# A hybrid delta-rule, attention and convolution trunk: value transposes one place later, and the weight splits of the first projection in mid-chunk

## What is computed

```
qkv_a, z_a, b_a, g_a, q_b, k_b, v_b, z_b = split_sizes(h @ w_in, AB_SIZES)
qkv_a = silu(causal_depthwise_conv(qkv_a, conv_w))
n_mat = where(strict, (k*beta) @ k.T * gamma, 0)          # 64 x 64 in each chunk of tokens
sol   = triangular_solve(eye + n_mat, [v*beta, k*beta*exp(decay)])
u, w  = sol[..., :dv], sol[..., dv:]
v_new = u - w @ state ;  o = q_dec @ state + qk @ v_new   # chunk after chunk
state = state * chunk_decay + k_dec.T @ v_new
```

## Time and profile before

| what | value |
|---|---|
| median of 3 runs | 2443.97 us (2443.47 to 2444.28) |
| span of the profiled execution | 2442.8 us; the launch's own time lies about 1.2 us above it (by the median) |
| TensorE busy | 2388.3 us, 98% of the span |
| DVE, ACT, GpSimd busy | 1294.1, 810.8, 229.8 us |
| longest chain | PE 83%, DVE 8%, issue 4%, ACT 2%, DMA 2% |
| DMA | 94 GB/s over the span |

### The profile page before, as it was taken

One profiled execution on the slowest core, in us unless ns is written; L12 is line 12 of the kernel. 1 busy time (PEld: TensorE's weight loads), 2 busy tenths in 40 slices (PEclk: granted clock), 3 DMA queues, 4 the chain that ended last, 5 costly groups with the idle time before them and its releaser, 6 DMA issues.

```text
span 2442.8 us, 29646 instructions
## 1 busy us (share of the span) xinstructions
PE 2388.3 (98%) x11652; PEld 1984.9 (81%) x11652; DVE 1294.1 (53%) x1725; ACT 810.8 (33%) x1377; POOL 229.8 (9%) x161
## 2 busy tenths in 40 slices
PE   7999999999999999999999999999999999999998
PEld 6788888888777878988777788888888888888776
DVE  5665656563555557643385783344333343433755
ACT  4233333332443436532244432212221222322434
POOL 3010101010010101001140420000000000001400
PEclk9999999999999999999999999999999999999999
DMA  6632333343433434452222233332323322333222
GB/s 174 109 70 67 76 68 75 66 77 70 123 91 73 83 73 131 149 180 96 93 70 69 78 97 94 103 103 81 108 86 103 103 95 86 95 104 121 69 69 86
DMA packets 237516, 229.80 MB, mean 94 GB/s; under 512 B 22384, under 2 KB 230768, under 8 KB 237424
## 3 DMA queue, kind: packets, MB, share of 16 engines
q1 hardware_dynamic: 236224, 226.96, 34.0%
q10 hardware_dynamic: 1200, 1.57, 0.2%
HBM read 223.52 MB, written 4.98 MB: 94 GB/s over the span
## 4 chain that ended last, share of the span: by engine, by line
PE 83%; DVE 8%; issue 4%; ACT 2%; DMA 2%; SPq 1%; POOL 0%; DVEq 0%; ACTq 0%; POOLq 0%
PE acc L887 22%; PE acc L889 21%; PE acc L888 21%; PE acc L1216 2%; PE acc L1217 2%; PE acc L1221 2%; DVE weights_lo L1353 2%; DMA weights_raw<-in_ab_w_in 1%; PE m L1036 1%; ACT weights_hi L460 1%; DVE work L1834 1%; PE acc L1089 1%; PE acc L1090 1%; PE acc L1091 1%; PE m L966 1%
## 5 line engine op out<-in xcount | busy, mean ns | idle before, releaser
L887 PE MATMUL acc<-input_hi,weights_hi 128*128 128x512 f32 (+1 forms) x2776 | 1092.1, 393 | 16.1 <-DVE weights_lo L1353 14.7
L889 PE MATMUL acc<-input_hi,weights_lo 128*128 128x512 f32 (+1 forms) x2776 | 1069.9, 385 | 0.0
L888 PE MATMUL acc<-input_lo,weights_hi 128*128 128x512 f32 (+1 forms) x2776 | 1069.0, 385 | 0.0
L1353 DVE TENSOR_TENSOR weights_lo<-weights_raw,weights_hi 128x1024 fp32r<-128x1024 f32 x400 | 533.5, 1348 | 320.8 <-ACT weights_hi L460 319.5
L887 PEld LDWEIGHTS acc<-input_hi,weights_hi 128*128 128x128 f32 x2776 | 523.4, 189 | 129.6 <-issue 16.0
L460 ACT ACTIVATE weights_hi<-weights_raw 128x1024 fp32r<-128x1024 f32 x400 | 418.5, 1057 | 622.6 <-PE acc L889 567.2
L889 PEld LDWEIGHTS acc<-input_hi,weights_lo 128*128 128x128 f32 x2776 | 522.7, 188 | 105.5
L888 PEld LDWEIGHTS acc<-input_lo,weights_hi 128*128 128x128 f32 x2776 | 523.7, 189 | 99.8 <-issue 1.9
L2051 POOL TENSOR_TENSOR small<-small 128x4 f32<-128x4 f32 (+1 forms) x19 | 24.5, 1288 | 824.1 <-DVE small L1583 378.1
L1778 DVE COPY work<-acc 128x512 f32<-128x512 f32 x48 | 31.1, 684 | 126.3 <-PE acc L889 115.8
L2113 POOL TENSOR_TENSOR work<-work 128x512 f32<-128x512 f32 x42 | 54.3, 1293 | 335.5 <-ACT work L742 332.5
(11 more groups left out here) (286 smaller groups left out, 2225.0 us busy)
## 6 DMA issues: line engine op xcount, KB each, us to landing
weights_raw<-in_c_w_in SPq DMA_DIRECT2D x128, 512.0 KB, 3.8
weights_raw<-in_ab_w_in SPq DMA_DIRECT2D x126, 512.0 KB, 5.2
weights_raw<-in_m_w_kv SPq DMA_DIRECT2D x32, 512.0 KB, 3.5
weights_raw<-in_ab_w_out SPq DMA_DIRECT2D x32, 512.0 KB, 4.3
weights_raw<-in_m_w_q SPq DMA_DIRECT2D x32, 512.0 KB, 3.4
weights_raw<-in_c_w_out SPq DMA_DIRECT2D x32, 512.0 KB, 4.1
residual<-in_x SPq DMA_DIRECT2D x32, 256.0 KB, 5.6
weights_raw<-in_m_w_o SPq DMA_DIRECT2D x16, 512.0 KB, 3.5
```

What stands on the lines that cost most here:

```text
L887: pe.matmul(out, w_hi[:, o:o + P], hi(kt), start=kt == 0, stop=False)
L888: pe.matmul(out, w_hi[:, o:o + P], lo(kt), start=False, stop=False)
L889: last = pe.matmul(out, w_lo[:, o:o + P], hi(kt), start=False, stop=kt == last_kt)
L1353: TTO(w_lo[:, s * CW:(s + 1) * CW], raw[:, c * CW:(c + 1) * CW], w_hi[:, s * CW:(s + 1) * CW].bitcast(F32), ALU.subtract).then_inc(lo_read ...
```

## The change

Two edits. The slot list: e1 goes ahead of vb, so that vb stands at slot 18, between e1 (16) and e2 (19); all other hops keep their slots. The splits: in all rounds but round 0 chunk c + 3 is split behind quarter 1 of chunk c (behind slot 4c+1), where chunk c + 2 was split at the start of chunk c; so split g moves from ahead of slot 4(g-2) to behind slot 4(g-3)+1. Round 0 keeps its places and does one split more at its end.

```
-D_HOPS = (["tr", "dk", "qb", "vb", "e1", "e2", "e5"] + ...
+D_HOPS = (["tr", "dk", "qb", "e1", "vb", "e2", "e5"] + ...
-D_PLACES = {"tr": 5, "dk": 6, "qb": 2, "vb": 2, "e1": 3, "e2": 8, ...
+D_PLACES = {"tr": 5, "dk": 6, "qb": 4, "e1": 2, "vb": 1, "e2": 8, ...
@@ ScalarE, ab_round
                 for c in range(16):
-                    split(C_AB + 16 * like + c + AHEAD, it - like)
+                    if like == 0:
+                        split(C_AB + c + AHEAD)
+                        if c == 15:
+                            split(C_AB + c + AHEAD + 1)
...
                         if k == 1:
                             convolved(c)
+                            split(C_AB + 16 * like + c + AHEAD + 1, it - like)
@@ VectorE, ab_round
-                    split(C_AB + 16 * like + c + AHEAD, it - like)
+                    if like == 0:
+                        split(C_AB + c + AHEAD)
+                        if c == 15:
+                            split(C_AB + c + AHEAD + 1)
...
                         evacuated(c, k)
+                        if k == 1:
+                            split(C_AB + 16 * like + c + AHEAD + 1, it - like)
```

More of the change, by code:

```diff
@@ L102, in last @@
         return self.sem, self.i * self.book.get("/", 0) + self.n
-D_HOPS = (["tr", "dk", "qb", "vb", "e1", "e2", "e5"] + [f"{x}{s}" for s in (4, 5) for x in ("p", "y")]
+D_HOPS = (["tr", "dk", "qb", "e1", "vb", "e2", "e5"] + [f"{x}{s}" for s in (4, 5) for x in ("p", "y")]
           + ["uw"] + [f"{x}{c}" for c in range(T // CH) for x in ("r", "s")] + ["ft"])
@@ L128, in placed @@
     return at_
-D_PLACES = {"tr": 5, "dk": 6, "qb": 2, "vb": 2, "e1": 3, "e2": 8, "e5": 2, "p": 1, "y4": 3, "y5": 2, "uw": 2,
+D_PLACES = {"tr": 5, "dk": 6, "qb": 4, "e1": 2, "vb": 1, "e2": 8, "e5": 2, "p": 1, "y4": 3, "y5": 2, "uw": 2,
             "r": 1, "s0": 2, "s2": 2, "s4": 2, "s6": 2, "s": 1, "s7": 4}
```

## The result

The changed kernel takes 2466.22 us (median of 5 runs, 2464.89 to 2466.94); the kernel before, run beside it on the same chip, takes 2443.97 (2442.16 to 2446.41). The ratio is 1.009, with an interval of 1.0079 to 1.0101: 22 us slower. The forecast was 2463.5, with a range of 2449 to 2470, and slower at 0.85. The direction and the place were right. Of the five terms of the sum, the one for p4 was taken 3.5 us too large and the one for the clock 5 us too small, and the one for the memory chunks had the wrong sign. The attention rounds, put at nothing, lost and gained some 3 us each. One statement of the prediction (that the value transposes' place is worth nothing) is false in the changed kernel.

The account below looks back on a forecast made before the run. Up to p4 a delta round is set by a chain through DVE, ACT and SP, not TensorE. Terms 16.8 + 2.8 - 2.7 - 1.2 + 4 = 19.7 us on 2443.97 gave 2463.5, range 2449 to 2470.

Parts of the forecast that it names:

- e2: DVE hop behind `take_z` in a delta round, for the second answer; forecast to start 2.9 us later against e1.
- Steps 1 to 3: Delta round up to the second answer: displaced splits make `n_t` 1.2, e1 1.3 and line 1503 4.2 us later.
- milder: Rival: GpSimd's mask does not hold the split and the clock stays; 8.1 us slower, 2452; chance 0.18.
- it only moves waits: Rival: earlier high half and extra wait cancel, p4 keeps its time, only scan and memory chunks change; 2442.9; chance 0.07.
- faster: Rival: displaced splits go into DVE's idle time, TensorE's waits at p4 and the transposes go; -9.9, 2434; chance 0.08.
- Step 4: P4 in four delta rounds: the whole 4.2 us delay lands on TensorE, with the DRAM way unchanged; 16.8 us slower.
- Step 5: At r0 and s0 in the delta rounds: a split ahead of the answer to r0 makes `v_new` late; +2.8 us.
- Step 6: At s4 in the delta rounds: the split ahead of `v_new` goes behind s4; -2.7 us.
- Step 7, attention: Attention rounds: ACT and DVE do the splits between the same two answers as before; 0.
- Step 7, memory chunks: Memory chunks: the 1.8 us wait for a weight's low half goes, the DVE stretch being one split shorter; -1.2 us.
- Step 8: TensorE's clock falls around the longer p4 wait in each delta round; +4 us in all, bounds 0 and 6.4.
- The value transposes are no gain by themselves: Ahead of p4 in delta rounds: TensorE time saved there, 0.96 us for these transposes, only changes its wait at p4.

Follow-up runs that it names:

- the later mask: Changed kernel, but GpSimd makes its second mask only after the second answer (solved inverses) instead of after the query answer: 2455.00 us, ratio 1.0042.
- the last kernel: Kernel before with new hop order, GpSimd's second mask after the second answer, and mid-chunk splits only from chunk 10 on in these rounds: 2437.86 us, ratio 0.9972.

## Why the prediction came out as it did

**Steps 1 to 3, the way to the second answer: right.** `n_t` came 1.0 us later (1.2 predicted), TensorE waited 0.8 for it, e1 came 1.0 later (1.3), and from e1 to the solved inverses it took 3.0 us more (2.9): 4.0 in all for 4.2. The split ahead of dk, the mask and the split ahead of e2 are each shown by an experiment that takes that one back alone. For the split beside the mask I took the upper bound, by the Trainium skill's rule in "SBUF — State Buffer", section "SBUF: two separate sides", that the port pair of DVE and GpSimd is locked for a whole instruction. The trace agrees: 3.15 us against 1.23 without the mask, and an end 1.1 us behind the mask's. The rival *milder* fell with it, and *it only moves waits* and *faster* fell with the waits for ACT of 1.05 and 1.76 us.

**Step 4, p4, 16.8: mis-sized, 13.3.** In rounds 2 and 3 p4 came 3.9 and 4.1 us later. In rounds 1 and 4 it was 3.3 and 1.9, because the way of the inverses through DRAM, which I took as the same after, was shorter. For line 375 the spread from issue to landing, is after:

```profile
DMA to landing us min/median/max: 3.3/3.3/4.0
```

The 5.5 us landing of the earlier trace rows was round 4's, so the kernel before had a wait of its own there that vanished. The prediction carried 1 us a round for this in its range; 2 were wanted in one of them.

**Step 5, s0, +2.8: 2.2. Step 6, s4, -2.7: -2.9.** As described; in round 4 s0 has only 0.2 of the loss.

**Step 7, attention, 0: -0.5, by luck.** The prediction has ACT and DVE do the displaced splits between the same two answers as before, so that no wait changes. The waits do change. The kernel before waits 2.06 us at 784.21 and its clock falls behind that the earlier trace rows; the kernel after waits 0.38 us there and its clock stays, which gives back 3.3 us. Then it waits at two places where the kernel before does not, for ACT (line 584) and for DVE (line 1582, 0.65 us), and loses 2.7 us again. TensorE of the kernel after, then a window over the first of these waits and what follows it:

```profile
804.74 0.49 PE L1040 MATMUL m<-work 64*128 64x128 f32 x4 [0.38 <-DVE residual L1594]
...
814.73 0.49 PE L1048 MATMUL m<-work 128*128 128x128 f32 x2 [1.49 <-ACT work L584]
```

```profile
803.00:812.00 9.00, 8.62 (x41) 6.29 (x40) 6.37 (x13) 2.81 (x6) 0.00 (x0) 1.00 0.58 111
```

The kernels of this record whose attention rounds have all splits in mid-chunk show the same three waits, and those with all of them at the chunk's start show the old one; no run undoes one of them alone.

**Step 7, memory chunks, -1.2: wrong, +0.4.** I had the wait at the weight's low half going because DVE's work ahead was one split shorter. The timeline after shows what stands ahead of that split now:

```profile
954.27 1.28 DVE L1624 TENSOR_TENSOR work<-acc,rstd_rows 128x512 f32<-128x512 f32 x2
955.47 1.22 DVE L1567 TENSOR_TENSOR work<-work 128x1024 f32<-128x1024 f32 x1
956.73 1.23 DVE L1569 TENSOR_TENSOR work<-work 128x1024 f32<-128x1024 f32 x1
957.87 1.22 DVE L1357 TENSOR_TENSOR weights_lo<-weights_raw,weights_hi 128x1024 fp32r<-128x1024 f32 x1
...
959.14 0.39 PE L891 MATMUL acc<-input_hi,weights_hi 128*128 128x256 f32 x1 [2.04 <-DVE weights_lo L1357]
```

Its high half is ready at 956.7, but DVE does the evacuation and two large multiplies first, which stood behind the split before. TensorE waits 2.04 us where it waited 1.8. The clock falls behind this wait in both kernels, and for longer after. The windows are of the kernel before, then of the kernel after:

```profile
934.60:938.00 3.40, 3.40 (x19) 3.40 (x18) 3.37 (x4) 2.77 (x6) 0.00 (x0) 0.50 0.52 161
```

```profile
960.30:967.10 6.80, 5.65 (x27) 5.35 (x26) 5.66 (x10) 4.40 (x6) 1.61 (x1) 0.50 0.72 228
```

That is read from the traces; no run here undid this part alone. The kernels with mid-chunk splits at this place wait 2.0 us here, those with the old places 1.8. The 0.5 us behind the memory chunks is a difference of single profiles that I don't explain.

**Step 8, the clock, +4: mis-sized, 9.0,** above its own bound of 6.4. I priced a fall by the one behind the 2.06 us wait (1.6 us), with part of it within the wait. Behind the waits of 4.0 to 4.9 us the granted clock was 0.50 for longer, 6.8 us in three rounds and 3.4 in the fourth, most of it in work: 2.0, 2.6, 2.7 and 1.6 us a round. Filling the wait took all of it away. The length of the wait alone does not set the price: in the run with the split of chunk 1 behind dk three waits of 3.6 to 4.5 us were followed by a loss of 1.5 us each. In the run with the later mask, whose waits at p4 were 2.1 to 3.1 us, a fall cost 1.5 us a round, near the price I had taken a fall from.

**"The value transposes are no gain by themselves", and what TensorE saves ahead of p4 only changes its wait there: false in the changed kernel.** It holds for p4's start, which the two kernels share to 0.2 us, and for the kernel before with the new order (ratio 1.0001), whose waits at p4 of 1.2 to 2.6 us had no fall behind them. But two waits with work between them, the fall of the clock lying ahead of slack, became one wait with the fall behind it, and that made 7.5 of the 9 us between the two kernels. Not taken up in the prediction at all: which side of the slack a slow stretch falls on.

The misses of -3.5 at p4, -0.6 at s0, -0.2 at s4, -0.5 in attention, +1.6 in the memory chunks, +5 at the clock, +0.5 behind the memory chunks and +0.7 ahead of the first round (again a difference of single profiles that I don't explain) add up to 3. That the total came so close, 2463.5 for 2466.2, is in part luck with their signs.

## What to carry to other kernels

Work moved ahead of a reply is paid on that reply, so look at each reply that the moved step now stands before, and ask which of its own inputs makes it wait there; a single split in the wrong place was worth 18 of 22 us here. When TensorE must wait for a chain anyway, look at the clock behind that wait before you remove a small wait ahead of it. Here two waits, or one filled with work, cost 7.5 to 9 us less than one wait of 4 to 4.9 us with the clock low in the work behind it; where the joined wait was 1.2 to 2.6 us, joining cost nothing. And before two-input DVE work is put anywhere, see what GpSimd does at that moment.

## What was not expected of the hardware

- The runs give no length of wait from which the clock falls. A single wait at p4 of 2.49 us (split of chunk 4 behind e2), of 2.30 us (the last kernel) and of 2.1 to 3.1 us (the later mask) had a fall behind it; waits at p4 of 2.09 us (the kernel before), 2.60 us (the new order alone) and 2.62 us (the new order with the later mask) had none.
- A slow stretch of TensorE costs only what lies outside slack: the same granted clock of 0.50 over 3.4 us cost nothing at 405.7 in the kernel with the splits alone, and 1.5 us at 299.9.
- The write of the inverses takes 3.3 us in most rounds, and in the fourth 5.5 before and 7.25 with the new order and the later mask, but 3.3 after. During the write of the fourth round the DMA engines were busy for a share of 0.60 to 0.78 before, and of 0.25 to 0.28 after (windows of 2 us from 528 to 534 and from 553 to 557). Whose transfers they were, and whether they hold the write up, stays open.
